# The expert-output stage in two passes over halves of the model's columns, with high and low gate parts in one product

## The chip, the cores and the metric

The kernel runs on one core of a Trainium2 chip. The metric is device time in microseconds (us) for one execution of the whole program; lower is better. Times below are either medians of several runs or come from one profiled execution, and each is marked as such. The engines are called TensorE (PE in the profile; its weight loads are listed apart as PEld), VectorE (DVE), ScalarE (ACT), GpSimd (POOL) and SyncE (SP), which here only issues transfers.

## The reference, cut to what matters

The program is one decoder layer for 256 tokens with 2048 model columns: a mixer of attention and retention heads, cross-attention into a memory, and then a feed-forward part with 128 x 128 = 16384 experts. Only this last part is changed.

```python
s1, i1 = lax.top_k(s[:, :, 0], 16)        # 128 keys on either side, 8 heads
s2, i2 = lax.top_k(s[:, :, 1], 16)
...                                       # 16 experts per head and token, softmax gates gb
u = jnp.take(expert_u, eb, axis=0)
act = jax.nn.gelu(jnp.einsum('tkd,td->tk', u, xb), approximate=False)
v = jnp.take(expert_v, eb, axis=0)
y = jnp.einsum('tk,tkd->td', gb * act, v)
...
return rmsnorm(x + y, final_norm_gain)
```

For 224 of the 256 tokens the kernel does not gather. It multiplies by the whole tables: `act` for all 16384 experts (the U stage), times a gate that is zero for experts that were not picked, and then times the whole table `v` (the V stage). The last 32 tokens are done the sparse way, with rows gathered from both tables.

## The kernel before, in words

All weights stream from memory in pieces of 128 partitions x 1024 f32 (512 KB): 180 pieces for the front, 256 of `u`, 256 of `v` (numbered from `V0`). A piece passes through a fixed chain. SyncE loads it into one of four `raw` slots (`load`, L360) once the piece four before it has been split. ScalarE copies it to `whi`, which keeps the high part only (`high_v`, L638), once TensorE has used the piece three before it (semaphore `used`; `whi` and `wlo` have three slots). The low part `wlo = raw - whi` is made by GpSimd in the front, the U stage and the first eight V pieces (L404), and by VectorE in the rest of the V stage (L1310 in `v_step`). Products of high and low parts together give close to f32 accuracy, and the low-by-low product is left out.

In the V stage the stationary operand is a 128 x 128 block of the piece and the moving operand is a row of gates for one key, 224 tokens wide. The gate matrix `W` (128 keys x 224 tokens on each partition) is split like the weights: ScalarE makes `gate_hi` (`gated_high`, L641) and VectorE `gate_lo` (L1313). The pieces run key by key, and for each key first the left and then the right half of the model's columns. So one pair of gate parts serves two pieces. Each of the 8 blocks of a piece takes three products of 224 columns: high weights by high gates (L1785), high weights by low gates (L1786), low weights by high gates (L1787). All 16 blocks of 224 columns accumulate over all keys in the 8 banks of PSUM, two to a bank.

Beside the pieces, three other kinds of work run in the V stage:
- GpSimd issues 128 gathers of `u` rows and 128 of `v` rows (`gather_group`, L420; each 128 partitions x 512 f32, 256 KB) into a ring of 16 row slots. Eight of them lie in `gather_low` and eight in `x2_back`, which must first have given back the residual `x2`.
- VectorE takes one row at a time: `u_row` (L1325) and `v_row` (L1337), placed by a rule on the piece number in the loop over `j` behind `v_step(j)`: 4 `u` rows every 3 pieces, 8 `v` rows every 7 pieces.
- After 24 pieces TensorE adds the residual by 32 calls (L1819; 64 instructions, since it is a plain f32 product), and at piece 121 it folds the sparse sums (L1831).

At the end all 16 blocks are squared by ScalarE and VectorE, summed over partitions by TensorE (L1860), turned into an inverse root by VectorE (L1396 to L1402), and scaled by the gain block by block (L1407), with an output transfer after each four blocks (L395).

The order on each engine is the order in which the code is written. No scheduler changes it, and engines meet only at semaphores.

## Time and profile before

| | before |
|---|---|
| median of 3 runs | 1999.95 us (1996.71 to 2000.69) |
| the profiled execution: its own time | 1985.34 us |
| the profiled execution: span of the trace | 1983.5 us |
| mean granted TensorE clock | 0.997 of full |
| busy share of the span: PE, PEld | 99%, 93% |
| busy share: DVE, ACT, POOL | 67%, 46%, 69% |
| bytes moved | 450.69 MB, mean 227 GB/s |
| V stage: first to last product | 1266.4 to 1964.7 us |

The U stage takes about 585 to 1264 us of the span and the V stage 1266 to 1965 us; some 19 us of closing work follow. A busy PE share of 99% says that TensorE nearly always had an instruction running, not that it streamed at its peak: the matmul rows overlap, so what one instruction costs in a dense stretch is read from the distance between starts. The trace leaves numbers out of names: `x2_back` reads `x_back` there, and most small tiles lie inside one called `big`.

### The profile page before, as it was taken

Reading aid. Unit: us, or ns where it says so; the run is one execution under the profiler, and the core shown is the slowest. Engines: PE = TensorE matmul, PEld = TensorE weight load, DVE = VectorE, ACT = ScalarE, POOL = GpSimd, SP = SyncE. Lnnn points to the kernel's source line nnn. Section 1 sums busy time; section 2 is a strip of 40 time slices with the busy share of each in tenths; the row PEclk is TensorE's granted clock in tenths of the full one; section 3 lists DMA queues with packets and bytes.
Section 4 is the critical chain, followed back from the end, with each engine's and each line's share of the span. In section 5 each row is a group of like instructions: output and inputs, shape, how many; then the busy total and the mean of one; then the engine's idle time right before and its main releaser. Section 6 shows DMA issues by size and latency. Waiting matters only on the chain.

```text
span 1983.5 us, 38782 instructions
## 1 busy us (share of the span) xinstructions
PE 1955.4 (99%) x13920; PEld 1843.1 (93%) x13920; DVE 1326.7 (67%) x2423; ACT 911.6 (46%) x1198; POOL 1361.0 (69%) x704
## 2 busy tenths in 40 slices
PE   8999999999999999999999999999999999999997
PEld 6888888888999999999999999999999999999997
DVE  6544683155536778778888886257888867777865
ACT  6453354474444444544444444433444444444443
POOL 7866768877888999988888888807555514444400
PEclk9999999999999999999999999999999999999998
DMA  8645656555765666666666666779999979999863
GB/s 326 191 138 151 200 149 223 182 179 161 228 186 181 206 207 209 198 199 192 191 193 196 191 191 192 246 247 330 328 328 322 333 239 316 304 306 310 308 198 115
DMA packets 126109, 450.69 MB, mean 227 GB/s; under 512 B 16464, under 2 KB 17104, under 8 KB 124880
## 3 DMA queue, kind: packets, MB, share of 16 engines
q1 hardware_dynamic: 101520, 365.76, 58.1%
q0 software_dynamic: 20480, 67.13, 9.7%
q10 hardware_dynamic: 4032, 16.76, 2.3%
q8 instruction: 50, 0.82, 0.2%
q14 instruction: 27, 0.22, 0.0%
HBM read 445.39 MB, written 4.19 MB: 227 GB/s over the span
## 4 chain that ended last, share of the span: by engine, by line
PE 56%; POOL 31%; issue 12%; DVE 1%; POOLq 0%; DMA 0%; ACT 0%; DVEq 0%
POOL wlo L404 30%; PE ps L1707 13%; PE ps L1785 11%; PE ps L1786 11%; PE ps L1787 11%; PE ps L1709 6%; PE ps L1720 1%; PE ps L1819 0%; POOLq L403 0%; PE ps L1860 0%; DVE big L1407 0%; DMA x_back<-in_u_rows,big 0%; POOL x_back L420 0%; POOLq L407 0%; DVE big L1398 0%
## 5 line engine op out<-in xcount | busy, mean ns | idle before, releaser
L404 POOL TENSOR_TENSOR wlo<-raw,whi 128x1024 fp32r<-128x1024 f32 x444 | 1077.2, 2432 | 206.0 <-ACT whi L466 189.9
L466 ACT ACTIVATE whi<-raw 128x1024 fp32r<-128x1024 f32 x436 | 461.7, 1060 | 637.8 <-PE ps L1709 361.3
L1707 PE MATMUL ps<-x_parts,whi 128*128 128x448 f32 x2048 | 654.6, 376 | 1.3 <-POOL wlo L404 1.3
L1785 PE MATMUL ps<-gate_hi,whi 128*128 128x224 f32 x2048 | 563.5, 275 | 3.9 <-DVE wlo L1310 2.3
L1786 PE MATMUL ps<-gate_lo,whi 128*128 128x224 f32 x2048 | 563.2, 275 | 0.0
L1787 PE MATMUL ps<-gate_hi,wlo 128*128 128x224 f32 x2048 | 563.1, 275 | 0.0
L1709 PE MATMUL ps<-x_parts,wlo 128*128 128x224 f32 x2048 | 540.8, 264 | 0.0
L638 ACT ACTIVATE whi<-raw 128x1024 fp32r<-128x1024 f32 x256 | 271.7, 1061 | 386.2 <-PE ps L1787 374.3
L1707 PEld LDWEIGHTS ps<-x_parts,whi 128*128 128x128 f32 x2048 | 384.6, 188 | 34.4 <-ACT big L592 1.1
L1310 DVE TENSOR_TENSOR wlo<-raw,whi 128x1024 fp32r<-128x1024 f32 x248 | 303.9, 1226 | 160.5 <-ACT whi L638 160.0
L1785 PEld LDWEIGHTS ps<-gate_hi,whi 128*128 128x128 f32 x2048 | 393.7, 192 | 4.3 <-DVE wlo L1310 2.5
L1787 PEld LDWEIGHTS ps<-gate_hi,wlo 128*128 128x128 f32 x2048 | 393.8, 192 | 0.0
L1786 PEld LDWEIGHTS ps<-gate_lo,whi 128*128 128x128 f32 x2048 | 393.7, 192 | 0.0
L1709 PEld LDWEIGHTS ps<-x_parts,wlo 128*128 128x128 f32 x2048 | 391.3, 191 | 0.0
L1426 PE MATMUL ps<-whi,x_parts 128*128 128x512 f32 (+1 forms) x544 | 214.5, 394 | 6.6 <-DVE x_parts L762 4.3
L1428 PE MATMUL ps<-whi,x_parts 128*128 128x512 f32 (+1 forms) x544 | 210.5, 387 | 0.0
L1427 PE MATMUL ps<-wlo,x_parts 128*128 128x512 f32 (+1 forms) x544 | 209.2, 385 | 0.0
L420 POOL DMA_INDIRECT gather_low<-in_w_v,big x64 | 72.3, 1130 | 107.5 <-DVE big L1337 87.7
L1107 DVE TENSOR_REDUCE big<-ps 128x224 f32<-128x448 f32 x128 | 79.3, 620 | 94.4 <-PE ps L1709 94.0
L420 POOL DMA_INDIRECT x_back<-in_u_rows,big x64 | 72.1, 1127 | 87.4 <-PE ps L1819 44.5
L1426 PEld LDWEIGHTS ps<-whi,x_parts 128*128 128x128 f32 x544 | 102.8, 189 | 30.6 <-DVE x_parts L762 6.4
L1428 PEld LDWEIGHTS ps<-whi,x_parts 128*128 128x128 f32 x544 | 102.6, 189 | 21.8
(242 smaller groups left out, 2298.5 us busy)
## 6 DMA issues: line engine op xcount, KB each, us to landing
raw<-in_w_u SPq DMA_DIRECT2D x256, 512.0 KB, 3.5
raw<-in_w_v SPq DMA_DIRECT2D x256, 512.0 KB, 4.7
raw<-in_w_front SPq DMA_DIRECT2D x180, 512.0 KB, 3.6
big<-in_x_t ACTq DMA_DIRECT2D x4, 512.0 KB, 9.4
big<-in_x ACTq DMA_DIRECT2D x4, 512.0 KB, 7.3
big<-in_mem ACTq DMA_DIRECT2D x4, 512.0 KB, 7.1
big<-in_mem_t ACTq DMA_DIRECT2D x2, 1024.0 KB, 6.1
big<-in_x ACTq DMA_DIRECT2D x2, 1024.0 KB, 6.7
```

Source lines behind the costliest of these rows:

```text
L404: nc.gpsimd.tensor_tensor(wlo[:, j % SPL, :], raw[:, j % RAW, :], whi[:, j % SPL, :], ALU.subtract).then_inc(lo_done, 1)
L466: nc.scalar.activation(whi[:, j % SPL, :], raw[:, j % RAW, :], ACT.Copy).then_inc(hi_done, 1)
L638: nc.scalar.activation(whi[:, (V0 + j) % SPL, :], raw[:, j % RAW, :], ACT.Copy).then_inc(hi_done, 1)
L1310: nc.vector.tensor_tensor(wlo[:, s, :], raw[:, j % RAW, :], whi[:, s, :], ALU.subtract).then_inc(lo_v_done, 1)
L1426: nc.tensor.matmul(out_ap, sh, mh, start=start, stop=False)
L1427: nc.tensor.matmul(out_ap, sh, ml, start=False, stop=False)
L1428: return nc.tensor.matmul(out_ap, sl, mh, start=False, stop=stop)
L1707: nc.tensor.matmul(sums[:, 0:2 * TD], whi[:, s, cols], x_parts[:, :, m, 0:TD], start=m == 0, stop=False, skip_group_check=True)
L1709: ins = nc.tensor.matmul(sums[:, TD:2 * TD], wlo[:, s, cols], xh[:, m, 0:TD], start=False, stop=m == DC - 1, skip_group_check=True)
L1785: nc.tensor.matmul(out, whi[:, s, cols], gate_hi[:, g, 0:TD], start=opens, stop=False, skip_group_check=True)
L1786: nc.tensor.matmul(out, whi[:, s, cols], gate_lo[:, g, 0:TD], start=False, stop=False, skip_group_check=True)
L1787: ins = nc.tensor.matmul(out, wlo[:, s, cols], gate_hi[:, g, 0:TD], start=False, stop=last, skip_group_check=True)
```

## The change

1. The table `v` is laid out so that all 128 keys of the left half come first (pieces 0 to 127) and then all 128 keys of the right half (128 to 255). A piece is as large as before.
2. One half has 8 blocks, one to a PSUM bank. A bank now holds a block twice, 448 columns: the products with high gates in one half of the bank and those with low gates (and of low weights by high gates) in the other. So the first product moves both gate parts at once (448 columns, L1837) and the second moves high gates against low weights (224 columns, L1839).
3. Both gate parts are made for every piece (`gated_high`, and `v_step` at L1349), since each key now comes back in the second pass. They lie side by side in `gate_parts`, which has three slots.
4. Between the passes VectorE adds the two halves of each bank into `FIRST` (L1380), and TensorE opens each bank of the second pass only after that (`first_joined`). The squares of `FIRST` are summed during the second pass, and ScalarE applies the gain to `FIRST` in the last four pieces.
5. The residual is loaded and added in two halves, after 24 pieces and after 132. The ring of gathered rows has 12 slots with a semaphore each; its last four lie in the half of `x2_back` that the first residual does not use. Rows are taken 50 per 41 pieces (`u`, from piece 14) and 25 per 21 pieces (`v`, from piece 132, or 140 behind the first eight).
6. At the end VectorE joins the 8 banks into `SECOND`, ScalarE squares them, TensorE sums 9 products instead of 16, and the final scaling covers 8 blocks with gain on VectorE, 5 blocks on GpSimd and 3 blocks in one VectorE instruction.

```diff
-        gate_hi = sb("gate_hi", [P, 2, T], F32R)
-        gate_lo = sb("gate_lo", [P, 2, T], F32R)
+        gate_parts = sb("gate_parts", [P, SPL, 2, TD], F32R)
...
-        x2_back = sb("x2_back", [P, TB, D])
+        x2_back = sb("x2_back", [P, 2, TB, PW])
...
+        ROW = [FOURS[k // 4][:, k % 4, :] for k in range(RING)]
+        FIRST = x2_back[:, 0].rearrange("p a b -> p (a b)")[:, 0:8 * TD].rearrange("p (a b) -> p a b", a=8)
...
@@ gpsimd
-            for g in range(GROUPS):
-                gather_group(0, g, u_rows)
-            for g in range(GROUPS):
-                gather_group(1, g, v_rows)
+            def gather_u(d):
+                if d >= RING:
+                    pool.wait_ge(rows_taken, d - RING + 1)
+                gather(d % RING, u_rows, IDX[0][:, d:d + 1])
+
+            def gather_v(e):
+                if e < 8:
+                    pool.wait_ge(rows_taken, P // RING * RING + e + 1)
+                if e == 8:
+                    pool.wait_ge(residual_in, 2)
+                if e >= RING:
+                    pool.wait_ge(rows_taken, P + e - RING + 1)
+                gather(e % RING, v_rows, IDX[1][:, e:e + 1])
...
+            for m in range(SPARE_BLOCKS):
+                ins = nc.gpsimd.tensor_tensor(OUT[:, m, :], FIRST[:, m, :], LAST_R, ALU.mult)
+            ins.then_inc(y_first, 1)
@@ scalar
-            def gated_high(k0, k):
-                nc.scalar.activation(gate_hi[:, k % 2, 0:TD], W[:, k0 + k, :], ACT.Copy).then_inc(ghi_done, 1)
+            def gated_high(k0, j):
+                nc.scalar.activation(gate_parts[:, j % SPL, 0, :], W[:, k0 + j, :], ACT.Copy).then_inc(ghi_done, 1)
...
-                    if j % 2 == 0:
-                        gated_high(i * CHUNKS_PER_BODY, j // 2)
+                    gated_high(i * BODY, j)
...
+                if j in (3, 4):
+                    load_back(1, j - 3)
...
+            for c in range(8):
+                act.wait_ge(second_joined, c + 1)
+                nc.scalar.activation(SQ[:, c, :], SECOND[:, c, :], ACT.Square).then_inc(sq_act, 1)
@@ vector
-                if j % 2 == 0:
-                    dve.wait_ge(ghi_done, j // 2 + 1)
-                    nc.vector.tensor_tensor(gate_lo[:, j // 2 % 2, 0:TD], W[:, j // 2, :],
-                                            gate_hi[:, j // 2 % 2, 0:TD], ALU.subtract).then_inc(glo_done, 1)
+                dve.wait_ge(ghi_done, j + 1)
+                nc.vector.tensor_tensor(gate_parts[:, j % SPL, 1, :], W[:, j % NK, :], gate_parts[:, j % SPL, 0, :],
+                                        ALU.subtract).then_inc(glo_done, 1)
...
+            def joined_block(c, to, done):
+                nc.vector.reduce_sum(to[:, c, :], ps[:, c, 0:2 * TD].rearrange("p (h t) -> p t h", h=2), AX).then_inc(done, 1)
...
+            for j in range(2, 2 * NK):
+                if j == NK + 1:
+                    first_block(0)
+                    first_block(1)
...
                 v_step(j, split=V0 + j >= POOL_END)
+                if j == NK + 1:
+                    for c in range(2, 8):
+                        first_block(c)
+                if j > NK + BODY and j % BODY == 0 and j // BODY - FOLD_BODY - 2 < 8:
+                    square_first(j // BODY - FOLD_BODY - 2)
...
-                while done[0] < P and j >= (14 if done[0] < 8 else 20) + done[0] * 3 // 4:
+                while done[0] < P and j >= taken_u(done[0]):
...
-                while done[1] < P and j >= FOLD_BODY * BODY + 7 + done[1] * 7 // 8:
+                while done[1] < P and j >= taken_v(done[1]):
...
+            for c in range(8):
+                dve.wait_ge(block_done, 7 + c + 1)
+                joined_block(c, SECOND, second_joined)
...
+            for k in range(2):
+                for c in range(4 * k, 4 * k + 4):
+                    ins = nc.vector.scalar_tensor_tensor(OUT[:, 8 + c, :], SECOND[:, c, :], GAIN[:, 5, 8 + c:9 + c], LAST_R,
+                                                         ALU.mult, ALU.mult)
                 ins.then_inc(y_out, 1)
...
+            nc.vector.tensor_tensor(OUT[:, rest, :], FIRST[:, rest, :],
+                                    LAST_R.unsqueeze(1).broadcast_to([P, 8 - SPARE_BLOCKS, TD]), ALU.mult).then_inc(y_out, 1)
@@ tensor
-                    nc.tensor.matmul(out, whi[:, s, cols], gate_hi[:, g, 0:TD], start=opens, stop=False, skip_group_check=True)
-                    nc.tensor.matmul(out, whi[:, s, cols], gate_lo[:, g, 0:TD], start=False, stop=False, skip_group_check=True)
-                    ins = nc.tensor.matmul(out, wlo[:, s, cols], gate_hi[:, g, 0:TD], start=False, stop=last, skip_group_check=True)
+            def v_block(s, c, first=False, last=False):
+                cols = slice(c * P, (c + 1) * P)
+                g = (s - V0) % SPL
+                nc.tensor.matmul(ps[:, c, 0:2 * TD], whi[:, s, cols], gate_parts[:, g].rearrange("p k t -> p (k t)"),
+                                 start=first, stop=False, skip_group_check=True)
+                return nc.tensor.matmul(ps[:, c, TD:2 * TD], wlo[:, s, cols], gate_parts[:, g, 0, :],
+                                        start=False, stop=last, skip_group_check=True)
...
+            residual(0)
             with pe.Fori(2, FOLD_BODY) as i:
...
+                    if j > last_first:
+                        pe.wait_ge(first_joined, c + 1)
+                    ins = v_block((V0 + j) % SPL, c, first=j > last_first, last=j == last_first)
...
+            residual(1)
...
+            for c in range(8):
+                v_block((END - 1) % SPL, c, last=True).then_inc(block_done, 1)
@@ the layout of the table
-    v = a["peer_v"][0].reshape(NK, NK, 2, PW).transpose(1, 2, 0, 3).reshape(2 * NK, P, PW)
+    v = a["peer_v"][0].reshape(NK, NK, 2, PW).transpose(2, 1, 0, 3).reshape(2 * NK, P, PW)
```

How the order of instructions changes is shown at three places. The first is TensorE in the middle of the V stage, before: the last block of one piece and the first of the next. `gate_hi`, `gate_lo` are the gate parts, `whi`, `wlo` the weight parts, `ps` is PSUM.

```order
L1785 MATMUL ps<-gate_hi,whi 128x224
L1786 MATMUL ps<-gate_lo,whi 128x224
L1787 MATMUL ps<-gate_hi,wlo 128x224
L1785 MATMUL ps<-gate_hi,whi 128x224 [waits lo_v_done,glo_done]
L1786 MATMUL ps<-gate_lo,whi 128x224
L1787 MATMUL ps<-gate_hi,wlo 128x224
L1785 MATMUL ps<-gate_hi,whi 128x224
```

And TensorE after, at the border between piece 127 and piece 128, where the second pass opens:

```order
L1837 MATMUL ps<-gate_parts,whi 128x448
L1839 MATMUL ps<-gate_parts,wlo 128x224
L1837 MATMUL ps<-gate_parts,whi 128x448 [waits first_joined,lo_v_done,glo_done]
L1839 MATMUL ps<-gate_parts,wlo 128x224
L1837 MATMUL ps<-gate_parts,whi 128x448 [waits first_joined]
L1839 MATMUL ps<-gate_parts,wlo 128x224
L1837 MATMUL ps<-gate_parts,whi 128x448 [waits first_joined]
L1839 MATMUL ps<-gate_parts,wlo 128x224
```

Three products of a block have become two, and in this one piece each block waits for the join of its bank; in every other piece only the first block waits, for `lo_v_done` and `glo_done`.

The second place is VectorE in the stretch of `u` rows, before, three pieces (ISA 128x512 is the row, ISA 128x1 the reading of its sum):

```order
L1325 ISA big 128x1
L1310 TENSOR_TENSOR wlo<-raw,whi 128x1024 [waits hi_done]
L1313 TENSOR_TENSOR gate_lo<-big,gate_hi 128x224 [waits ghi_done]
L1325 ISA x_back,big<-x_back,big 128x512
L1325 ISA big 128x1
L1310 TENSOR_TENSOR wlo<-raw,whi 128x1024 [waits hi_done]
L1325 ISA x_back,big<-x_back,big 128x512 [waits row_in3]
L1325 ISA big 128x1
L1325 ISA x_back,big<-x_back,big 128x512
```

And after, in the same stretch:

```order
L1347 TENSOR_TENSOR wlo<-raw,whi 128x1024 [waits hi_done]
L1349 TENSOR_TENSOR gate_parts<-big,gate_parts 128x224 [waits ghi_done]
L1355 ISA x_back,big<-x_back,big 128x512 [waits row_in9]
L1355 ISA big 128x1
L1347 TENSOR_TENSOR wlo<-raw,whi 128x1024 [waits hi_done]
L1349 TENSOR_TENSOR gate_parts<-big,gate_parts 128x224 [waits ghi_done]
L1355 ISA x_back,big<-x_back,big 128x512 [waits row_in10]
L1355 ISA big 128x1
L1347 TENSOR_TENSOR wlo<-raw,whi 128x1024 [waits hi_done]
L1349 TENSOR_TENSOR gate_parts<-big,gate_parts 128x224 [waits ghi_done]
```

Each piece now has its own low gate part, and each row has its own semaphore.

The third place is VectorE at pieces 128 to 130, before:

```order
L1310 TENSOR_TENSOR wlo<-raw,whi 128x1024 [waits hi_done]
L1313 TENSOR_TENSOR gate_lo<-big,gate_hi 128x224 [waits ghi_done]
L1337 SCALAR_TENSOR_TENSOR big<-gather_low,big 128x512 [waits rows_taken]
L1310 TENSOR_TENSOR wlo<-raw,whi 128x1024 [waits hi_done]
L1337 SCALAR_TENSOR_TENSOR big<-gather_low,big 128x512 [waits rows_taken]
L1310 TENSOR_TENSOR wlo<-raw,whi 128x1024 [waits hi_done]
L1313 TENSOR_TENSOR gate_lo<-big,gate_hi 128x224 [waits ghi_done]
L1337 SCALAR_TENSOR_TENSOR big<-gather_low,big 128x512 [waits rows_taken,row_in1]
```

And after:

```order
L1347 TENSOR_TENSOR wlo<-raw,whi 128x1024 [waits hi_done]
L1349 TENSOR_TENSOR gate_parts<-big,gate_parts 128x224 [waits ghi_done]
L1380 TENSOR_REDUCE x_back<-ps 128x224 [waits block_done] x2
L1347 TENSOR_TENSOR wlo<-raw,whi 128x1024 [waits hi_done]
L1349 TENSOR_TENSOR gate_parts<-big,gate_parts 128x224 [waits ghi_done]
L1380 TENSOR_REDUCE x_back<-ps 128x224 [waits block_done] x5
L1380 TENSOR_REDUCE x_back<-ps 128x224 [waits used]
L1347 TENSOR_TENSOR wlo<-raw,whi 128x1024 [waits hi_done]
L1349 TENSOR_TENSOR gate_parts<-big,gate_parts 128x224 [waits ghi_done]
```

The `v` rows have moved away from here, and the eight joins of the banks stand around the work of piece 129.

## Rows read from the trace of the kernel before

**Rows 1.** The profile's page: span, busy time (share) xinstructions, ScalarE's copies (count | busy, mean ns).
```profile
span 1983.5 us, 38782 instructions
...
PE 1955.4 (99%) x13920; PEld 1843.1 (93%) x13920; DVE 1326.7 (67%) x2423; ACT 911.6 (46%) x1198; POOL 1361.0 (69%) x704
...
L638 ACT ACTIVATE whi<-raw 128x1024 fp32r<-128x1024 f32 x256 | 271.7, 1061 | 386.2 <-PE ps L1787 374.3
```

**Rows 2.** Busy time in two stretches: stretch, length, engines (xinstructions), clock, DMA share, GB/s.
```profile
700.00:800.00 100.00, 99.67 (x630) 94.04 (x628) 79.24 (x206) 51.18 (x63) 93.92 (x40) 1.00 0.68 206
1400.00:1500.00 100.00, 100.00 (x898) 100.00 (x898) 81.77 (x157) 44.55 (x56) 57.02 (x52) 1.00 0.94 326
```

**Rows 3.** Waits in the V stage: engine, line, for whom: us, times, longest.
```profile
ACT whi L638 <- PE ps L1787: 374.3, 246, 8.5
DVE wlo L1310 <- ACT whi L638: 160.0, 215, 2.9
...
DVE x_back L1325 <- DMA x_back<-in_u_rows,big: 12.3, 1, 12.3
...
ACT whi L638 <- DMA raw<-in_w_v: 10.0, 6, 2.4
```

**Rows 4.** Timeline of TensorE, V stage: start, duration, engine, line, operation.
```profile
1420.15 0.28 PE L1785 MATMUL ps<-gate_hi,whi 128*128 128x224 f32 x1
...
1422.83 0.28 PE L1785 MATMUL ps<-gate_hi,whi 128*128 128x224 f32 x1
```

**Rows 5.** Timeline of TensorE in the U stage, blocks of one piece.
```profile
1000.38 0.38 PE L1707 MATMUL ps<-x_parts,whi 128*128 128x448 f32 x1
1000.60 0.27 PE L1709 MATMUL ps<-x_parts,wlo 128*128 128x224 f32 x1
...
1002.28 0.38 PE L1707 MATMUL ps<-x_parts,whi 128*128 128x448 f32 x1
```

**Rows 6.** Timeline of VectorE, a piece with two `u` rows.
```profile
1488.12 1.23 DVE L1310 TENSOR_TENSOR wlo<-raw,whi 128x1024 fp32r<-128x1024 f32 x1 [0.84 <-ACT whi L638]
1489.26 0.39 DVE L1313 TENSOR_TENSOR gate_lo<-big,gate_hi 128x224 fp32r<-128x224 f32 x1
1489.56 0.68 DVE L1325 CUSTOM_DVE_ANT_0 gather_low<-gather_low,big 128x512 f32<-128x512 f32 x1
...
1490.80 1.23 DVE L1310 TENSOR_TENSOR wlo<-raw,whi 128x1024 fp32r<-128x1024 f32 x1
```

**Rows 7.** Timeline of VectorE, a piece with two `v` rows.
```profile
1709.82 1.41 DVE L1337 SCALAR_TENSOR_TENSOR big<-x_back,big 128x512 f32<-128x512 f32 x2
1711.15 1.22 DVE L1310 TENSOR_TENSOR wlo<-raw,whi 128x1024 fp32r<-128x1024 f32 x1
```

**Rows 8.** Timeline of TensorE around a stall at 1346 us.
```profile
1348.41 0.40 PE L1785 MATMUL ps<-gate_hi,whi 128*128 128x224 f32 x1 [2.28 <-DVE wlo L1310]
...
1351.80 0.39 PE L1786 MATMUL ps<-gate_lo,whi 128*128 128x224 f32 x1
```

**Rows 9.** Busy time in stretches of 10 us, columns as in rows 2.
```profile
1360.00:1370.00 10.00, 10.00 (x92) 10.00 (x91) 8.58 (x18) 4.36 (x5) 7.87 (x8) 1.00 0.98 358
...
1380.00:1390.00 10.00, 10.00 (x92) 10.00 (x91) 7.84 (x16) 4.62 (x6) 7.80 (x7) 1.00 1.01 384
```

**Rows 10.** Timeline of VectorE: a join of 448 to 224 columns, and what follows it.
```profile
662.90 0.62 DVE L1107 TENSOR_REDUCE big<-ps 128x224 f32<-128x448 f32 x1 [2.41 <-PE ps L1709]
663.45 3.30 DVE L1162 TENSOR_TENSOR big<-big 128x256 f32<-128x256 f32 x2
```

**Rows 11.** Timeline of the end: sums over partitions, root, scaling, output.
```profile
1964.52 6.23 PE L1860 MATMUL ps<-big 128*128 128x224 f32 x32
...
1970.79 0.39 DVE L1396 TENSOR_SCALAR big<-ps 128x224 f32<-128x224 f32 x1 [3.59 <-PE ps L1860]
...
1975.54 5.10 DVE L1407 SCALAR_TENSOR_TENSOR big<-ps,big 128x224 f32<-128x224 f32 x14
1976.37 4.63 SPq L395 DMA_DIRECT2D out<-big  x4
```

More of the change, by code:

```diff
@@ L88, with issued_u, taken_u, issued_v @@
 FOLD_BODY, LAST_ROWS = 10, 242
+OPENING, SPARE_BLOCKS = 8, 5
+def issued_u(d):
+    return OPENING + d // 2 if d < RING else taken_u(d - RING) + 1
+def taken_u(d):
+    return 14 + d * 41 // 50
+def issued_v(e):
+    return 116 + e * 3 // 4 if e < 8 else 135 + (e - 8) // 2 if e < 12 else 137 + (e - 12) * 21 // 25
+def taken_v(e):
+    return 132 + e * 4 // 5 if e < 8 else 140 + (e - 8) * 21 // 25
 PAIRS_PER_BODY = 10
@@ L392, in _ @@
             sp.dma_start(out_rows, X_GAINED).then_inc(out_done, 16)
-            for k in range(4):
-                sp.wait_ge(y_out, k + 1)
-                sp.dma_start(out[:, 4 * k:4 * k + 4, :], OUT[:, 4 * k:4 * k + 4, :]).then_inc(out_done, 16)
+            for ready, count, m0, m1 in ((y_out, 1, 8, 12), (y_first, 1, 0, SPARE_BLOCKS), (y_out, 2, 12, 16), (y_out, 3, SPARE_BLOCKS, 8)):
+                sp.wait_ge(ready, count)
+                sp.dma_start(out[:, m0:m1, :], OUT[:, m0:m1, :]).then_inc(out_done, 16)
             sp.wait_ge(out_done, 80)
@@ new lines, in gather_v @@
+            def gather_v(e):
[6 more added lines that the diff above has]
+                gather(e % RING, v_rows, IDX[1][:, e:e + 1])
+            asked = [0, 0]
+            for j in range(OPENING, 2 * NK):
+                if j == OPENING:
+                    pool.wait_ge(picks, 1)
+                    pool.wait_ge(used, V0)
+                while asked[0] < P and j >= issued_u(asked[0]):
+                    gather_u(asked[0])
+                    asked[0] += 1
+                while asked[1] < P and j >= issued_v(asked[1]):
+                    gather_v(asked[1])
+                    asked[1] += 1
@@ L1328, in v_row @@
             def v_row(slot):
-                row = gathered(1, slot)
+                dve.wait_ge(row_in[slot % RING], 16 * ((P + RING - 1 - slot % RING) // RING + slot // RING + 1))
+                row = ROW[slot % RING]
                 weight = WEIGHTS[:, slot:slot + 1]
@@ L1796, in v_piece @@
                     pe.wait_ge(lo_v_done, n0 + (V0 - POOL_END + j + 1))
-                s, g, half = (V0 + j) % SPL, j // 2 % 2, j % 2
-                if first and j == 0:
-                    v_products(s, g, half, range(4, 8), True)
-                    pe.wait_ge(act_taken, NK)
-                    ins = v_products(s, g, half, range(4), True)
-                else:
-                    ins = v_products(s, g, half, range(8), first)
-                ins.then_inc(used, 1)
+            def v_piece(n0, j):
+                v_ready(n0, j)
+                for c in range(8):
+                    ins = v_block((V0 + j) % SPL, c)
+                ins.then_inc(used, 1)
@@ L1806, in _, with residual @@
+            def residual(h):
+                pe.wait_ge(x2_in, 32 * (h + 1))
+                for c in range(8):
+                    for tb, w in ((0, P), (1, TD - P)):
+                        ins = nc.tensor.matmul(ps[:, c, tb * P:tb * P + w], x2_back[:, h, tb, c * P:(c + 1) * P], ident[:, 0:w],
+                                               start=False, stop=False, skip_group_check=True)
+                ins.then_inc(residual_in, 1)
             pe.wait_ge(gated, TOK_PAIRS)
             pe.wait_ge(act_taken, NK - 2)
-            for j in range(BODY):
-                v_piece(0, 0, j, first=j < 2)
+            v_ready(0, 0)
@@ L1810, in _ @@
+            for c in (2, 3, 4, 5, 6, 7, 0, 1):
+                if c == 0:
+                    pe.wait_ge(act_taken, NK)
+                ins = v_block(V0 % SPL, c, first=True)
+            ins.then_inc(used, 1)
+            for j in range(1, BODY):
+                v_piece(0, j)
             with pe.Fori(1, 2) as i:
                 for j in range(BODY):
-                    v_piece(i * BODY, i * CHUNKS_PER_BODY, j)
-            pe.wait_ge(x2_in, 32)
-            for m in range(DC):
-                for tb, w in ((0, P), (1, TD - P)):
-                    c0 = m % 2 * TD + tb * P
-                    ins = nc.tensor.matmul(ps[:, m // 2, c0:c0 + w], x2_back[:, tb, m * P:(m + 1) * P], ident[:, 0:w],
-                                           start=False, stop=False, skip_group_check=True)
@@ L1845, in _ @@
                              start=False, stop=False, skip_group_check=True).then_inc(norm_folded, 1)
[L1846 to L1860 removed]
+            v_ready(0, 2 * NK - 3)
+            for c in (0, 1, 3, 4, 5, 6, 7, 2):
+                if c == 2:
+                    pe.wait_ge(var_ready, 10)
+                ins = v_block((V0 + 2 * NK - 3) % SPL, c)
+            ins.then_inc(used, 1)
+            v_piece(0, 2 * NK - 2)
+            v_ready(0, 2 * NK - 1)
+            for c in range(8):
+                v_block((END - 1) % SPL, c, last=True).then_inc(block_done, 1)
+            pe.wait_ge(ones_ready, 1)
+            pe.wait_ge(second_joined, 1)
+            nc.tensor.matmul(ps[:, 0, 0:TD], LAST_ONES, SUM_SQ, start=True, stop=False)
+            for c in range(8):
+                pe.wait_ge(sq_act, c + 1)
+                ins = nc.tensor.matmul(ps[:, 0, 0:TD], LAST_ONES, SQ[:, c, :], start=False, stop=c == 7)
             ins.then_inc(last_sums, 1)
```

175 lines of the change are left out of this document (77 added, 98 removed).

## The prediction

> **What bounds the kernel now.** I read the page first. TensorE is busy 99% of the span [rows 1], so the question is what its time in the V stage consists of and whether anything else would take over if it were shortened.
>
> The table of stretches says that in a dense 100 us of the V stage 898 products run at full clock, and that PE and PEld are both busy all of it [rows 2]. That is 111.4 ns from one product of 224 columns to the next. The timeline agrees: from the first product of a block to that of the block eight further on it is 1422.83 - 1420.15 = 2.68 us, 0.335 us a block [rows 4]. A piece of 8 blocks takes 2.67 us.
>
> The view of waits shows the others waiting for TensorE: ScalarE 374 us before its copies (`used`), VectorE 160 us for ScalarE [rows 3]. ScalarE waited for a load only 6 times, 10.0 us in all, at most 2.4 us. So in the V stage TensorE's own pace is the bound, and VectorE and the transfers come next: VectorE is 82% busy and the DMA engines 94%, at 326 GB/s, in the stretch of `u` rows [rows 2].
>
> **Part 1: two products for three.** The shape of the new pair (448 columns of high weights, then 224 of low weights) is already in this trace, in the U stage. There a block takes (1002.28 - 1000.38) / 6 = 0.317 us, of which 0.22 us is the step from the 448 to the 224 product and 0.10 us the step back [rows 5]; over 100 us 630 products make 315 pairs, again 0.317 us [rows 2]. U has the same two weight loads, data type and widths, so I take its pace. Against 3 x 111.4 = 334 ns this is 17 ns a block, and 256 x 8 = 2048 blocks give 35 us. The bounds: if the 448 product keeps its 0.215 us but the 224 product its 0.111 us of the V stage, the block costs 0.326 us and the gain is 17 us; if the reading of the 100 us stretch is off by one product in 630, the gain is 36 us.
>
> The Trainium skill (page "TensorE: Matmul & The Clock Gate", section "Back-to-back issue gap") puts the isolated distance between products at columns / 2.4 GHz plus 2.5 ns. By it joining two products saves 2.5 ns, some 5 us over the stage, an estimate from that page. The trace does not agree: 111.4 ns stands where that rule has 96 ns, and the pair's 317 ns where it has 285 ns.
>
> **Part 2: a stall that goes.** At 1346 us VectorE waited 12.3 us for the first gathered row in `x2_back` [rows 3], because that gather had to wait for the residual. TensorE then idled 2.28 us, and the next products stood (1351.80 - 1348.41) / 16 = 0.212 us apart, the lower clock, for 17 products [rows 8]: 2.3 + 17 x 0.10 = 4.0 us. In the changed kernel all 12 slots are free before the residual, so this goes: -4 us. What is late next there is only the opening burst below.
>
> **Part 3: the residual and the fold.** The 64 instructions of the residual become 32 and 32, nothing gained or lost. Its second load is issued by ScalarE at pieces 123 and 124 and used after 132, some 20 us later; cover enough. Both 0.
>
> **Part 4: VectorE's load per piece.** Before, a piece with two `u` rows runs from `wlo` to `wlo` in 1490.80 - 1488.12 = 2.68 us: 1.14 for `wlo`, 0.30 for the low gate part, 1.24 for the rows [rows 6]. After, every piece has the gate part and on average 50/41 = 1.22 rows: 1.14 + 0.30 + 1.22 x 0.62 = 2.20 us. With `v` rows, where two take 1711.15 - 1709.82 = 1.33 us [rows 7], it is 1.44 + 1.19 x 0.67 = 2.23 us. TensorE's piece will be 8 x 0.317 = 2.53 us, so 0.3 us is left on average. A piece with two rows takes 2.68 or 2.77 us and overruns by up to 0.24 us, which the next one gives back. A piece has (from `used` of three before) two pieces of time, 5.07 us, for ScalarE's copy of 1.06 us [rows 1], a `wlo` of 1.23 us [rows 6] and handovers, about 2.5 us: that hides it. Cost 0; without that cover each `u` stretch piece would cost up to 0.15 us.
>
> **Part 5: transfers.** A piece moves 0.524 MB and 1.22 rows of 0.262 MB, 0.844 MB in 2.53 us, 333 GB/s. From 1360 to 1390 us, three stretches of which the first and last are shown, the queues carried 358 to 384 GB/s with TensorE dense and at full clock [rows 9]. So it fits, with about a tenth to spare: 0. The opening is the tight place. All 12 first gathers are issued at once (before, eight), on top of the loads of pieces and of `x2`, where the six waits of ScalarE for loads lie now. Half of `x2` comes later, 1 MB, which is just the four more gathers. I take +1 us, bounds 0 and +5 (a stall like that of part 2 and a little more).
>
> **Part 6: the turn between passes.** TensorE must find bank c joined before it opens it for piece 128, and VectorE does the joins around piece 129. A join of 448 columns steps on after 663.45 - 662.90 = 0.55 us [rows 10]. From the start of piece 127: block 0 done 0.5, joins 0 and 1 until 1.65, then `wlo` and gate part of piece 129, 1.44 us, then joins 2 to 7, six times 0.55, until about 6.4, and the last block after it ends at 6.8 us. Undisturbed it would be 5.07 us. That is 1.8 us of waits in pieces of about 0.25 us, some of them longer; with a drop of the clock as in [rows 8] 3.5 us. I take +2.5, bounds 0 (if joins run further ahead) and +6.
>
> **Part 7: the end.** Now the sums over partitions run 6.2 us after the last product, the root chain starts at 1970.79, and 16 scalings of 0.365 us end at 1980.6 [rows 11]. After: eight joins at 0.55 us begin with the last piece's first block and end about 2.7 us behind its last product; one square and one product later, at 3.6, the root chain starts, 2.5 us sooner. The scaling takes 8 x 0.37 plus one instruction of 672 columns, near 0.8 us, in place of 5.8: 2.0 us. Together 4.5 us, but the four output transfers then stand closer than now, with 1.83 MB (128 x 3584 f32) to move in little more than 5 us at the rate of [rows 9]. I take -3, bounds 0 and -5.
>
> **The sum.** -35 - 4 + 1 + 2.5 - 3 = -38.5 us. On the profiled execution's own 1985.3 us that is 1946.8 us. The median of the runs stands 14.6 us above the profiled execution for a reason that the trace does not tell; I carry the difference over unchanged: 1999.95 - 38.5 = 1961.4 us.
>
> **Rivals.**
> - *The pair does not keep U's pace in V, or VectorE and the loads give it small waits.* With 0.326 us a block the sum is -20.5 and the time 1979 us. For it: VectorE goes to 88% busy by part 4. Against it: same instruction shapes, and rows 3 show no wait of TensorE for anything in steady state.
> - *A product costs its columns and next to nothing else.* That is what the skill's rule would mean: then joining saves about 5 us in place of 35, and the time is 1991 us. The distances of [rows 4, 5] speak against it.
> - *The transfers become the bound and the kernel gets slower.* The place is the 213 pieces with rows. To lose the 38.5 us again each must take 0.18 us more, 2.71 us, so the queues must carry under 0.844 / 2.71 = 311 GB/s. At 300 GB/s a piece is 2.81 us, +60 us, and the time is 2021 us. For it: 94% busy at 326 GB/s [rows 2]. Against it: [rows 9].
> - *The gain is larger:* the opening and the turn cost nothing and the end brings its 5 us: -44, 1956 us. I count this in the forecast's own range.
>
> **How the numbers follow.** Forecast 0.80, with its own range 1953 to 1970 us from the bounds of parts 5 to 7. The slower or partly fed pair 0.12 (1970 to 1985), columns only 0.03 (1991), transfers as the bound 0.05 (over 2000). The range 1953 to 1975 leaves out some 0.13 above and 0.05 below. A measurement of this kernel can tell about 0.2%, 4 us: faster 0.94, same 0.01, slower 0.05.
>
> **What would show it.** In a dense stretch of the V stage 630 products in 100 us, and starts 0.317 us apart from block to block; 0.326 would make the first rival right. No wait of VectorE for a row over 2 us and no idle TensorE near the 20th piece but for the opening. The queues near 333 GB/s with ScalarE waiting for `used` and seldom for a load; many waits for loads would be the third rival. At the turn six waits of TensorE for VectorE's joins, 2 us or less in sum, and the clock either still full or low for some us after. At the end under 17 us from last product to the end. The forecast is wrong if waits of TensorE for `wlo` or gate parts recur through the row stretches.

## The result, and the profile after

| | before | after |
|---|---|---|
| median of the runs with the result | 2000.28 us (4 runs, 1996.71 to 2000.69) | 1942.9 us (4 runs, 1940.5 to 1945.48) |
| ratio, with 95% interval | | 0.9717 (0.9701 to 0.9732) |
| measured again later, both on one chip | 1984.3 us (9 runs) | 1939.91 us (5 runs) |
| ratio there | | 0.9777 (0.9764 to 0.9791) |
| span of the profiled execution | 1983.5 us | 1940.4 us |

The change is worth 57 us by the first pair and 44 us by the second. The two traces differ by 43.1 us. I had forecast a gain of 38.5 us and a time of 1961.4 us, between 1953 and 1975 us; the measured time lies below that. The changed kernel is the same in both pairs within 3 us. What differs by 16 us between the pairs is the kernel before, and the experiments return to that.

The page of the changed kernel, to be held against [rows 1]; there are 3470 instructions fewer. Of products and of weight loads 2062 each went (2048 of them in the V stage's blocks), and other engines have some more:

```profile
span 1940.4 us, 35312 instructions
...
PE 1913.4 (99%) x11858; PEld 1767.5 (91%) x11858; DVE 1378.1 (71%) x2568; ACT 950.8 (49%) x1337; POOL 1396.1 (72%) x709
```

A dense stretch of the V stage (columns as in rows 2), to be held against the second row of [rows 2]:

```profile
1400.00:1500.00 100.00, 100.00 (x637) 94.86 (x635) 89.09 (x177) 53.30 (x80) 55.58 (x49) 1.00 0.95 335
```

VectorE went from 82 to 89% and the queues from 326 to 335 GB/s, and TensorE still had no gap. The waits in the V stage, against [rows 3]:

```profile
ACT whi L680 <- PE ps L1839: 287.4, 236, 4.8
...
DVE wlo L1347 <- ACT whi L680: 68.4, 136, 4.0
...
ACT whi L680 <- DMA raw<-in_w_v: 2.3, 2, 1.2
...
PE ps L1837 <- DVE gate_parts L1349: 1.8, 2, 1.6
```

The columns are microseconds in all, times, and the longest wait. VectorE's wait of 12.3 us for a gathered row is gone. ScalarE still waits for TensorE (287 us), so TensorE is still what the others wait for. VectorE waits 68 us for ScalarE, where it had 160.

The timeline of TensorE, 32 blocks apart, against [rows 4]:

```profile
1419.84 0.37 PE L1837 MATMUL ps<-gate_parts,whi 128*128 128x448 f32 x1
1420.06 0.26 PE L1839 MATMUL ps<-gate_parts,wlo 128*128 128x224 f32 x1
...
1429.95 0.37 PE L1837 MATMUL ps<-gate_parts,whi 128*128 128x448 f32 x1
```

A block takes (1429.95 - 1419.84) / 32 = 0.316 us. The piece with two `u` rows on VectorE, against [rows 6]:

```profile
1429.35 1.23 DVE L1347 TENSOR_TENSOR wlo<-raw,whi 128x1024 fp32r<-128x1024 f32 x1 [0.39 <-ACT whi L680]
1430.49 0.38 DVE L1349 TENSOR_TENSOR gate_parts<-big,gate_parts 128x224 fp32r<-128x224 f32 x1
...
1432.01 1.22 DVE L1347 TENSOR_TENSOR wlo<-raw,whi 128x1024 fp32r<-128x1024 f32 x1
...
1434.45 1.23 DVE L1347 TENSOR_TENSOR wlo<-raw,whi 128x1024 fp32r<-128x1024 f32 x1 [0.30 <-issue]
```

It takes 1432.01 - 1429.35 = 2.66 us, of the same parts as before. The next piece has one row, takes 2.44 us, and gives the overrun back.

TensorE's idle stretches within the V stage are few. These are one in the opening and the first of six at the turn:

```profile
1300.03 0.47 PE L1837 MATMUL ps<-gate_parts,whi 128*128 128x448 f32 x1 [1.02 <-issue]
```

```profile
1595.60 3.27 DVE L1380 TENSOR_REDUCE x_back<-ps 128x224 f32<-128x448 f32 x6
...
1596.28 0.19 PEld L1837 LDWEIGHTS ps<-gate_parts,whi 128*128 128x128 f32 x1 [0.65 <-DVE x_back L1380]
```

In the opening it was 1.0 us, and 0.3 us more shortly after. At the turn seven steps from the last undisturbed block (1595.42 to 1599.34 us) took 3.9 us where 2.2 are usual: 1.7 us, with the clock at full. The first of them took 0.85 us and the next five 0.53 us each, where 0.316 is usual.

The end, against [rows 11]:

```profile
1923.54 0.27 PE L1839 MATMUL ps<-gate_parts,wlo 128*128 128x224 f32 x1
...
1924.03 3.19 PE L1935 MATMUL ps<-big 128*128 128x224 f32 x16
1927.25 0.39 DVE L1447 TENSOR_SCALAR big<-ps 128x224 f32<-128x224 f32 x1 [1.27 <-PE ps L1935]
...
1931.28 4.98 DVE L1457 SCALAR_TENSOR_TENSOR big<-big 128x224 f32<-128x224 f32 x8
1931.42 3.87 POOL L470 TENSOR_TENSOR big<-x_back,big 128x224 f32<-128x224 f32 x5 [72.35 <-DVE big L1453]
1934.05 3.35 SPq L415 DMA_DIRECT2D out<-big  x4
1936.19 0.84 DVE L1462 TENSOR_TENSOR big<-x_back,big 128x672 f32<-128x672 f32 x1
```

Before, the last product of the V stage began at 1964.41 us:

```profile
1964.41 0.27 PE L1787 MATMUL ps<-gate_hi,wlo 128*128 128x224 f32 x1
```

The root chain now starts 3.7 us after the last product began, in place of 6.4. The scaling takes 5.75 us (1931.28 to 1937.03), nearly the 5.8 of before: VectorE's eight scalings with gain took 4.98 us, 0.62 us each. The span ends 3.4 us after the last scaling, where it was 2.9 us.

### The profile page after: what moved, and what is told of

The parts are those of the page before. It is cut to its first block, busy times and chain, and to the rows that moved or that the text cites. A ratio compares the mean times of both kernels' runs of the same rounds, so it can differ in the third digit from the quotient of the medians.

```text
span 1940.4 us, 35312 instructions
## 1 busy us (share of the span) xinstructions
PE 1913.4 (99%) x11858; PEld 1767.5 (91%) x11858; DVE 1378.1 (71%) x2568; ACT 950.8 (49%) x1337; POOL 1396.1 (72%) x709
## 4 chain that ended last, share of the span: by engine, by line
PE 55%; POOL 31%; issue 12%; DVE 1%; POOLq 0%; ACT 0%; DVEq 0%
POOL wlo L424 31%; PE ps L1837 22%; PE ps L1762 14%; PE ps L1839 11%; PE ps L1764 6%; PE ps L1775 1%; PE ps L1859 0%; POOLq L423 0%; DVE big L1457 0%; PE ps L1935 0%; DVE wlo L1347 0%; POOLq L427 0%; DVE x_back L1380 0%; DVE big L1449 0%; ACT whi L680 0%
## 5 line engine op out<-in xcount | busy, mean ns | idle before, releaser
L1837 PE MATMUL ps<-gate_parts,whi 128*128 128x448 f32 x2048 | 648.2, 375 | 3.2 <-DVE gate_parts L1349 1.8
L1839 PE MATMUL ps<-gate_parts,wlo 128*128 128x224 f32 x2048 | 542.8, 265 | 0.0
L1837 PEld LDWEIGHTS ps<-gate_parts,whi 128*128 128x128 f32 x2048 | 384.4, 188 | 38.5 <-issue 3.1
L1839 PEld LDWEIGHTS ps<-gate_parts,wlo 128*128 128x128 f32 x2048 | 391.2, 191 | 0.0
L434 POOL DMA_INDIRECT gather_low<-in_w_v,big x88 | 119.3, 1356 | 70.4 <-DVE big L1368 40.4
L434 POOL DMA_INDIRECT gather_low<-in_u_rows,big x88 | 103.8, 1180 | 75.1 <-DVE big L1355 62.7
L1482 PEld LDWEIGHTS ps<-wlo,x_parts 128*128 128x128 f32 x544 | 103.0, 189 | 20.3
L1349 DVE TENSOR_TENSOR gate_parts<-big,gate_parts 128x224 fp32r<-128x224 f32 x256 | 108.8, 425 | 4.1 <-ACT gate_parts L683 3.8
```

The costliest lines, as they stand in the source:

```text
L434: nc.gpsimd.indirect_dma_start(ROW[at_row], None, table, bass.IndirectOffsetOnAxis(index.bitcast(I32), 0)).then_inc(row_in[at_row], 16)
L1482: nc.tensor.matmul(out_ap, sh, ml, start=False, stop=False)
L1837: nc.tensor.matmul(ps[:, c, 0:2 * TD], whi[:, s, cols], gate_parts[:, g].rearrange("p k t -> p (k t)"), start=first, stop=False, skip_grou ...
L1839: return nc.tensor.matmul(ps[:, c, TD:2 * TD], wlo[:, s, cols], gate_parts[:, g, 0, :], start=False, stop=last, skip_group_check=True)
```

## The experiments

Each time is compared as a ratio to the kernel before, which was measured beside it on the same chip. That kernel stood at 1983.2 to 1984.4 us (medians) each time, on four chips. The ratio of the changed kernel, to hold the others against, is 0.9777 (0.9764 to 0.9791).

**The kernel before, unchanged.** No edit.

> The kernel before, unchanged, profiled once more. Its runs stood at 1996.7 to 2000.7 us while its profiled execution took 1985.3 us; the changed kernel's runs and profile agree (1940.5 to 1945.5). Theory A: the profiled execution of before was a fortunate one, and its usual execution loses 15 us somewhere in the V stage, most likely in the stretches with gathered rows where the queues stand at 94% busy: this profile shows a span near 1998 us and a V stage of about 713 us in place of 698. Theory B: the extra 15 us lies in the front or the U stage, and the V stage again takes 698 us. Theory C: a profiled execution is always some 15 us shorter than a timed one of this kernel: span near 1984 us again.

Measured: 1984.95 us (10 runs), span 1981.8 us. Its trace is like the first profile. TensorE stands idle for 2.1 us behind the late row (1.65 us of them in the stretch shown), where it was 2.3. The granted clock falls after that (0.97 in the mean of the stretch), and 898 products run in the 100 us behind it.

```profile
1345.00:1400.00 55.00, 53.35 (x463) 53.35 (x464) 45.46 (x88) 22.80 (x29) 42.09 (x36) 0.97 0.97 358
1400.00:1500.00 100.00, 100.00 (x898) 100.00 (x897) 81.19 (x157) 45.13 (x57) 56.50 (x50) 1.00 0.94 325
```

None of the three theories is what happened: timed and profiled executions agree, and both stand at 1984. Theory C (a profile is shorter than a timed run) falls. A and B could not be tried, since the 2000 us did not come back. The same kernel twice more, on two other chips:

> The kernel before, unchanged, in one more call. Of its runs 38 stood near 1984 us on two chips and 4 near 2000. If this call meets the condition of those four, its trace shows where the 16 us lie: in the V stage (theory A of the first call), or in the front or the U stage (theory B). If it stands near 1984 again, the 2000 us stay without a trace.

> The kernel before once more, for one profile: near 1984 us again, or at last near 2000 us with a trace that shows where the 16 us lie.

Measured: 1984.14 us (8 runs) and 1983.04 us (one run). With the runs beside the other kernels that is 75 executions on four chips, all from 1981.6 to 1986.9 us. So there is no trace of an execution near 2000 us.

The last of these traces shows something that the others don't. TensorE waited at the same place for 2.08 us, and the granted clock stayed at full (1.00, the third number from the end in the second row):

```profile
1347.74 0.37 PE L1785 MATMUL ps<-gate_hi,whi 128*128 128x224 f32 x1 [2.08 <-DVE wlo L1310]
```

```profile
1345.00:1400.00 55.00, 52.92 (x475) 52.74 (x474) 46.39 (x91) 23.72 (x30) 44.04 (x37) 1.00 0.96 358
```

It did 475 products in this stretch, against 463 in the trace above, which had waited as long and had then run at the lower clock.

**Three products again.**

```diff
-                nc.tensor.matmul(ps[:, c, 0:2 * TD], whi[:, s, cols], gate_parts[:, g].rearrange("p k t -> p (k t)"), ...
+                nc.tensor.matmul(ps[:, c, 0:TD], whi[:, s, cols], gate_parts[:, g, 0, :], start=first, ...
+                nc.tensor.matmul(ps[:, c, TD:2 * TD], whi[:, s, cols], gate_parts[:, g, 1, :], start=False, ...
```

> The changed kernel with one edit: high weights by high gates and high weights by low gates are two products of 224 columns again, everything else (two passes, ring, residual in halves, end) as changed. If the joined product brings the gain, 2048 blocks cost 0.335 us in place of 0.316: +39 us on 1942.9, about 1982 us. Rival: if the two passes, the ring and the end bring it, the time stays within 10 us of 1943. The difference between 1982 and the 2000 us of before is then what the rest of the change brings: 7 us by my parts 2 and 7, or 18 us if the rest also removes the 15 us that separate the timed runs of before from its profile.

Measured: 1979.54 us, ratio 0.9978 (0.9968 to 0.9987), against 0.9777 of the changed kernel. The joined product alone is worth 2.0% of 1984 us, 40 us (some 3 us either way), and the rest of the change 4.4 us (2.6 to 6.3). The rival is out. Joining two products takes away one product and one weight load for each block; which of the two brings the gain was not tried. The trace shows the old pace, with VectorE's new work in place:

```profile
1400.00:1500.00 100.00, 100.00 (x898) 100.00 (x898) 84.94 (x167) 49.78 (x75) 46.53 (x46) 1.00 0.93 314
```

**The stall alone, on the kernel before.**

```diff
-                while done[0] < P and j >= (14 if done[0] < 8 else 20) + done[0] * 3 // 4:
+                while done[0] < P and j >= (14 if done[0] < 8 else 24) + done[0] * 3 // 4:
```

> The kernel before with one edit: the u rows behind the first eight are taken four pieces later (24 in place of 20), so that VectorE should no longer wait for the first gathered row in x2_back while TensorE runs dry at 1346 us. By my part 2 this brings 4 us: 1996 us in the timed runs. If the 15 us between the timed runs and the profile of before also grow from that wait (a longer wait for the same row in most executions), it brings near 18 us: 1982 us. If neither, no change.

Measured: 1980.69 us, ratio 0.9985 (0.9976 to 0.9995), so 3.0 us with 1.0 to 4.8. The stall is gone from the trace, and 32 products more are done in the 55 us:

```profile
1345.00:1400.00 55.00, 55.00 (x495) 55.00 (x494) 43.34 (x84) 25.08 (x31) 37.98 (x34) 1.00 0.96 353
```

That agrees with the 4 us of part 2. It says nothing on the 2000 us, as the condition was absent.

**A gap between the gate parts.** `gate_parts` with 256 columns for each part and 224 used, as the `x` parts of the U stage lie.

```diff
-        gate_parts = sb("gate_parts", [P, SPL, 2, TD], F32R)
+        gate_parts = sb("gate_parts", [P, SPL, 2, T], F32R)
...
-                ... gate_parts[:, g].rearrange("p k t -> p (k t)"),
+                ... gate_parts[:, g, :, 0:TD],
```

> The changed kernel with one edit: each gate part takes 256 columns of space with 224 used, so the moving operand of 448 columns is two runs of 224 with a gap of 32 between, as the x parts of the U stage are apart, in place of 448 in a row. A block took 0.3157 us in the V stage of the changed kernel and 0.3167 us in the U stage. If the layout makes that difference, 2048 blocks cost 2 us more, 1945 us. If not, no change: 1943 us.

Measured: 1941.83 us, ratio 0.9787 (0.9771 to 0.9804). The interval overlaps with that of the changed kernel, so the times do not tell. The trace does, by a little:

```profile
1400.00:1500.00 100.00, 100.00 (x634) 94.60 (x633) 88.81 (x177) 53.00 (x79) 55.51 (x48) 1.00 0.96 335
```

```profile
1420.13 0.38 PE L1837 MATMUL ps<-gate_parts,whi 128*128 128x448 f32 x1
...
1429.95 0.38 PE L1837 MATMUL ps<-gate_parts,whi 128*128 128x448 f32 x1
```

31 blocks in 9.82 us are 0.3168 us each, U's pace; without the gap 0.3159. So the gap costs 0.9 ns a block, 2 us over the stage. Over all undisturbed steps of the stage the means are 0.3168 us in this trace and 0.3157 to 0.3158 us in the seven traces without the gap.

**The changed kernel again,** unedited.

> The changed kernel, unedited, timed beside the kernel before in one call on one chip. In the first call before took 1983.9 us on a chip where the variant with a gap took 1941.8; my theory now is that the 2000 us of before belong to a chip or a time, not to the kernel's stages, and that the change is worth what the two traces show, 43 us: if before stands near 1984 here, this one is at 1941 (ratio 0.978). Rival: before keeps 1984 in one call and 2000 in another while the changed kernel always takes 1942, so that the gain is 42 or 58 us depending on the chip; then before is near 2000 here with this one still near 1942.

Measured: 1939.91 us beside 1984.3 us. Ratio 0.9777 (0.9764 to 0.9791): 44 us, as the two traces say. That the 2000 us belong to a chip or a time is not shown by it, as they did not come back.

**The last scaling on VectorE alone.**

```diff
-            for m in range(SPARE_BLOCKS):
-                ins = nc.gpsimd.tensor_tensor(OUT[:, m, :], FIRST[:, m, :], LAST_R, ALU.mult)
...
-            nc.vector.tensor_tensor(OUT[:, rest, :], FIRST[:, rest, :],
-                                    LAST_R.unsqueeze(1).broadcast_to([P, 8 - SPARE_BLOCKS, TD]), ALU.mult).then_inc(y_out, 1)
+            for rest in (slice(0, 4), slice(4, 8)):
+                nc.vector.tensor_tensor(OUT[:, rest, :], FIRST[:, rest, :],
+                                        LAST_R.unsqueeze(1).broadcast_to([P, 4, TD]), ALU.mult).then_inc(y_out, 1)
```

> The changed kernel with one edit: the last scaling is all on VectorE (eight blocks with gain, then two instructions of four blocks), none on GpSimd. In the trace the eight scalings took 4.98 us, 0.62 us each, while GpSimd worked beside them; alone they took 0.365 us each before. If the two engines slow one another, VectorE alone needs 8 x 0.37 + 2 x 1.1 = 5.1 us against 5.75 us now: 0.6 us sooner, and the outputs leave in even steps: 1 to 2 us less. Rival: GpSimd's share is real help and this ends 1 us later.

Measured: 1938.74 us, ratio 0.9769 (0.9756 to 0.9782), not to be told from the changed kernel. The trace:

```profile
1930.21 2.99 DVE L1451 SCALAR_TENSOR_TENSOR big<-big 128x224 f32<-128x224 f32 x8
1933.11 2.09 DVE L1456 TENSOR_TENSOR big<-x_back,big 128x896 f32<-128x896 f32 x2
```

The same eight scalings take 2.99 us alone and 4.98 us with GpSimd at work. Eight more blocks on VectorE then cost 2.09 us. The whole takes 4.99 us against 5.75: 0.8 us less in the trace, where 0.6 was expected. The 1 to 2 us in all cannot be told from nothing by the times.

**More work for VectorE.**

```diff
+                if j >= 8:
+                    dve.wait_ge(extra_done, j - 8)
+                    nc.vector.tensor_tensor(EXTRA, W[:, j % NK, :], gate_parts[:, j % SPL, 0, :], ALU.subtract).then_inc(extra_done, 1)
```

> The changed kernel with one instruction more per piece on VectorE from piece 8 on: a subtraction of 224 columns like the low gate part, into space that nothing reads. It steps VectorE on by 0.30 us, so a piece with 1.22 rows costs it 2.50 us of TensorE's 2.53. If my account of VectorE (2.20 of 2.53 us) holds, the steady pieces still fit and the cost is small, 0 to 6 us in all (a little more at the turn and in pieces with two rows). Rival: VectorE was already nearly the bound; then 213 pieces with rows pay 0.2 us and more each, over 40 us.

Measured: 1945.25 us, ratio 0.9803 (0.9788 to 0.9818), 5 us more than the changed kernel. The stretch with `u` rows still holds; that with `v` rows has VectorE at 99.9% and TensorE losing 1.4 us in 100:

```profile
1400.00:1500.00 100.00, 100.00 (x636) 94.86 (x635) 99.55 (x218) 53.47 (x80) 73.42 (x49) 1.00 0.96 334
1700.00:1800.00 100.00, 98.58 (x617) 92.03 (x616) 99.86 (x169) 52.13 (x78) 83.37 (x47) 1.00 0.95 320
```

So my account of VectorE held: about 0.3 us a piece was free, and with that spent the stage starts to suffer.

The extra work also slowed GpSimd. In the stretch from 1400 to 1500 us both kernels issue 49 gathers of `u` rows, which took 1.17 us each in the changed kernel and 1.53 us here:

```profile
L436 POOL DMA_INDIRECT gather_low<-in_u_rows,big x32 | 47.1, 1473 | 16.9 <-DVE big L1360 14.8 <-issue 2.1
```

**Denser rows.**

```diff
-    return 14 + d * 41 // 50
+    return 14 + d * 2 // 3
...
-    return 132 + e * 4 // 5 if e < 8 else 140 + (e - 8) * 21 // 25
+    return 132 + e * 4 // 5 if e < 8 else 140 + (e - 8) * 2 // 3
```

> The changed kernel with one edit: gathered rows are taken three for every two pieces (u and v, behind the first eight v) in place of 1.2 a piece. While rows are taken a piece then moves 0.524 + 1.5 x 0.262 = 0.917 MB in 2.53 us, 363 GB/s, and VectorE steps 2.37 (u) or 2.44 us (v) of 2.53. If the queues really carry 358 to 384 GB/s beside a dense TensorE, as rows 9 showed for 30 us, the time stays within 4 us of 1940. Rival: 330 GB/s is what they carry for long; then 157 pieces pay up to 0.25 us each and the time rises by 20 to 40 us.

Measured: 1947.26 us, ratio 0.9817 (0.9801 to 0.9834), 8 us more. Neither theory holds for both stretches:

```profile
1400.00:1500.00 100.00, 100.00 (x636) 94.86 (x635) 95.07 (x200) 53.52 (x80) 77.31 (x58) 1.00 0.98 363
1700.00:1800.00 100.00, 97.41 (x611) 91.23 (x610) 95.24 (x139) 50.90 (x76) 83.55 (x54) 1.00 0.95 337
```

With `u` rows the queues carry 363 GB/s and TensorE loses nothing. With `v` rows they carry 337, VectorE waits for gathered rows (13 times, 6.7 us in the whole stage), and TensorE loses 2.6 us in 100. But their busy share is lower there, 0.95 for 0.98, so they are not shown to be what is short. GpSimd, which issues the gathers, is at its limit:

```profile
L434 POOL DMA_INDIRECT gather_low<-in_w_v,big x37 | 58.6, 1583 | 11.3 <-issue 9.1 <-DVE big L1368 2.1
L434 POOL DMA_INDIRECT x_back<-in_w_v,big x17 | 25.9, 1522 | 5.2 <-DVE big L1368 2.7 <-issue 2.4
```

These 54 gathers between 1700 and 1800 us took 1.56 us each and stand back to back, with 0.3 us between each and the next, as wherever GpSimd has no wait. That is one every 1.85 us. Three rows for two pieces ask for one every 2.53 / 1.5 = 1.69 us, and in the stretch of `u` rows, where a gather took 1.34 us, that is what the trace has. In the changed kernel GpSimd was busy 60 us of the same 100 and waited 32 us for free slots. Part 5 was right that 333 GB/s fit, and its tenth to spare is shown for `u` only; what ran out for `v` was an engine that the part does not name.

**The opening spaced out** (with the scaling on VectorE).

```diff
+                elif d >= 4:
+                    pool.wait_ge(used, V0 + 5 + d)
```

> The kernel e4 (scaling all on VectorE) with one more edit: the fifth to twelfth of the first gathers are issued one per piece (behind used of V0 + 5 + d) in place of all at once. TensorE lost 1.3 us at 1300 us in the opening of the changed kernel, where the queues carried 395 GB/s. If the burst of gathers is the cause, that goes: 1 to 1.5 us less than e4. Rival: the loads of x2 and the gain rows cause it, and the time does not move.

Measured: 1939.07 us, ratio 0.9771 (0.9758 to 0.9784): no gain over e4. ScalarE still waited 6 times for loads in the opening, 9.0 us, and no wait of TensorE is left there. But the changed kernel's second trace had no idle TensorE there either, and e4's had one step of 0.89 us, so the 1.3 us are not in every execution, and their cause stays open.

**All joins first** (with the scaling on VectorE).

```diff
                 if j == NK + 1:
-                    first_block(0)
-                    first_block(1)
+                    for c in range(8):
+                        first_block(c)
...
-                if j == NK + 1:
-                    for c in range(2, 8):
-                        first_block(c)
```

> The kernel e4 (scaling all on VectorE) with one more edit: at the turn all eight joins stand ahead of the work of piece 129, in place of two ahead and six behind. The turn of the changed kernel cost TensorE 1.7 us in six waits behind joins 2 to 7. With all joins first, piece 128 should find its banks nearly in time (block 7 at 5.0 us after the start of piece 127, against 6.5) and piece 129 then waits for its low parts until about 6.4: 1.3 us lost in one wait instead of 1.7 us in six. So 0.4 us less than e4 (ratio 0.9767), not to be told apart in the times, but to be seen in the trace. Rival: one wait of over 1 us drops the clock and costs 1.5 us more.

Measured: 1938.36 us, ratio 0.9777 (0.9764 to 0.9791). At the turn one wait takes the place of six:

```profile
1590.54 4.34 DVE L1374 TENSOR_REDUCE x_back<-ps 128x224 f32<-128x448 f32 x8 [0.16 <-PE ps L1830]
...
1596.37 0.19 PEld L1828 LDWEIGHTS ps<-gate_parts,whi 128*128 128x128 f32 x1 [1.14 <-DVE gate_parts L1343]
```

It is 1.3 us lost in all, as expected, and the clock did not fall. The gain is too small for the times. Of the variants none beats the changed kernel beyond its interval. The gap, the scaling on VectorE, the spaced opening and the early joins cannot be told from it; the extra work and the denser rows are slower.

## Why the prediction was wrong

**The step that failed is the one from the trace to the median.** "I carry the difference over unchanged: 1999.95 - 38.5 = 1961.4 us." The difference of 14.6 us was in the kernel before only, and only in its first runs. The changed kernel stood at 1942.9 us with the result and at 1939.9 later, so it carried none or 3 us of it. The profiled execution of before (1985.34 us) is none of those first timed runs, and it agrees with all the 75 later ones; the sum belonged on it alone. There it gave 1946.8 us, 5 us above the changed kernel's own profiled execution (1942.2 us) and 7 us above its later median. Where the 16 us between 2000 and 1984 lie was not found, and what caused them stays open. If both kernels met the same condition, the front and the U stage, which are the same code, hold at most 3 us of it and the rest is in the V stage or the end of the kernel before. That is argued, not shown.

The range had no place for this. By the prediction's own bounds of parts 5 to 7 the time runs from 1956 to 1972 us, not from 1953 to 1970 as it says, and neither leaves room for the 14.6 us to be missing after the change.

**Part 1, the joined product, was undersized:** 35 us against 40 by the experiment. By the traces a block went from 0.335 to 0.3159 us. From 1352.14 us to the end of the stage 1826 blocks of before start, 0.3351 us apart if two longer steps (0.71 and 0.48 us) are counted as usual ones. 0.0192 x 2048 is 39 us. I had read 0.334 off the count of products in 100 us, which counts the ones at both edges, although [rows 4] said 0.335: 2 us. And U's 0.317 is the pace of two runs of 224 columns with a gap: 2 us. The bound of 17 us and the rivals "does not keep U's pace" and "columns only" are out. The Trainium skill's rule for the isolated distance (page "TensorE: Matmul & The Clock Gate", section "Back-to-back issue gap") would have given 5 us. The measured 40 us are not that, and the section itself says that its rule comes out too low for narrow products that each bring a weight load.

**Part 2, the stall,** was right: 3.0 us (1.0 to 4.8) for a forecast of 4. Its 1.7 us for the lower clock are not in every execution: one of four traces of the kernel before has the wait without the drop.

**Part 3** was right: the residual's halves cost nothing that shows.

**Part 4, VectorE,** was right in its cost of 0 and in what is left, 0.3 us a piece, shown by spending it.

**Part 5, transfers,** was right in steady state, though it did not ask what the gathers cost GpSimd. The opening cost 1.3 us in one execution and none in the next, for +1.

**Part 6, the turn:** the working gave 1.8 us of waits and the trace has 1.7. The clock did not fall, so the 0.7 us that I added were not needed.

**Part 7, the end,** gave 2.2 us by the traces (from the last product's start to the end 16.9 us for 19.1) against 3. The sums came 2.7 us sooner for 2.5. The scaling gained nothing in place of 2.0 us, since the scalings beside GpSimd took 0.62 us in place of 0.37; I had set the two side by side without asking what they do to each other.

**The slower case** did not come: the queues carried 335 GB/s in the stretch that I named.

## What to carry to other kernels

A trace prices a change; it does not explain why the runs shown stand elsewhere, and a difference between the two that has no row belongs into the range (here its full 15 us on the low side) and not silently into the forecast. Where products of 224 columns stand 111 ns apart, a block of three costs 335 ns, and moving two parts under one stationary operand in one product saved 19 ns of it. That is 6% of a block, and there are 2048 of them. Before work is given to a second engine near the end, ask what it costs the first one. And when transfers are priced by their rate, price the engine that issues them too.

## What the runs showed of the hardware

- VectorE's scaling of 128 x 224 steps on in 0.37 us alone and in 0.62 us while GpSimd multiplies beside it (2.99 us and 4.98 us for eight).
- A moving operand of 448 columns in one run gave 0.3159 us a block and one of 2 x 224 with a gap of 32 gave 0.3168 us, with the same second product.
- An idle TensorE of 2.28 us was followed by products 0.212 us apart at the lower clock [rows 8], and so were those of 2.1 and 2.3 us in two more traces of this kernel. In a fourth, 2.08 us at the same place were not. Nor were the turn's six waits (0.5 us and then 0.2 us each), nor the one of 1.1 us with all joins first.
- The queues carried 363 GB/s beside a dense TensorE with rows of `u`. With rows of `v` at the same density they carried 337 GB/s, while GpSimd issued gathers back to back, one every 1.85 us.
- GpSimd's gather of 128 rows of `u` took 1.17 us with VectorE 89% busy and 1.53 us with one more subtraction a piece on VectorE (99.6% busy). With three rows for two pieces it took 1.34 us for `u` and 1.56 us for `v`. Why they differ was not tried. GpSimd's spans are rough, but the starts 1.85 us apart agree with them.
